# Two blocks of a language model on one core: another opening, index scores and gate panel moved, and marks that hold GpSimd

## The chip, the cores and the metric

The kernel runs on one core of a Trainium2 chip. The metric is the device time of one execution in microseconds (us), the median of the runs shown. All arithmetic is fp32; the large products are made of rounded halves, as told below.

## The reference

Input x has 512 tokens of 1024 features. Block 1 normalises x, projects it with w_in, and merges three branches: gated linear attention in chunks of 64, a causal convolution, and windowed attention. Block 2, run twice with weights of its own, has two branches: a gated recurrence (HGRN) and an attention over keys that a small indexer selects. Every block ends in a feed-forward part.

```
u = rmsnorm(x, g_mix);  z = u @ w_in                                  # block 1
y = sigmoid(gates) * (branches @ their own output weights);  h = x + merged @ w_o
# block 2, for each of two layers: z = rmsnorm(h) @ w_in_2
rel   = relu(einsum('bqhd,bsd->bqhs', rope(iq), rope(ik)))            # 4 index heads of 64
score = einsum('bqh,bqhs->bqs', iw, rel), causal
idx   = top_k(score, 128)                                             # per query
attn  = softmax(q k over idx) v,  q and k normed per head and roped
hgrn  = gated recurrence per head; rms over the head's 128 values, times silu(gate)
h    += (sigmoid(g1) * (attn @ w1) + sigmoid(g2) * (hgrn @ w2)) @ w_out
h    += (silu(h' @ w_a) * (h' @ w_b)) @ w_down,  h' = rmsnorm(h)
```

## The kernel before, in words

**Data.** Activations lie transposed, features on partitions (xT, 8 chunks of 128 x 512 tokens). Every operand of a large product is split in a high half (rounded to the format fp32r) and a low half (the rest), and a product is three matmuls: high x high, low x high, high x low. A weight panel is up to 2048 columns per partition (1 MB). The list of panels is written out by hand in weight_panels (line 190). SyncE loads a panel into one of three buffers raw when the panel that had the buffer has been used (line 917). ScalarE casts it to its high half wh (line 956) wherever its program calls ahead() (line 950); ahead() casts every further panel whose buffer's last user is an earlier pair than the one ScalarE has come to. GpSimd subtracts to get the low half wl, in four pieces of 512 columns, panel after panel in order (line 940). project (line 470) makes 48 matmuls of 128x512, 24 for each of two output chunks, into one of two PSUM pairs; a pair is free again when ScalarE or VectorE has read it. Each project can be cut in 4 steps of 12 matmuls.

**Opening.** x arrives as tokens, TensorE turns its 8 chunks (line 853), VectorE copies them to xT. ScalarE scales each chunk to the high half vh and squares it (squares, line 996), VectorE makes the low half vl_first (line 1500) and adds up squares (gather, line 1483 on). TensorE waits until all chunks are copied (line 858), then projects two panels from x scaled by the gains but not yet normalised (opening, line 535), and makes the column sums of the squares (sum_squares, line 518) behind the last chunk of the first panel. ScalarE's root and VectorE's reciprocal (line 1520) give scale. shadow (lines 1048 and 1535) then makes the normalised x chunk by chunk: VectorE scales a chunk (line 1538), ScalarE copies it to uh (line 1054), VectorE subtracts to get ul (line 1477). The first two panels' results are multiplied by scale as they are read (line 2075). The third panel (gla rank, gaT) and all others use uh and ul.

**Cores.** core (line 543) and core_chunked (line 620) run 8 units, each of 128 tokens and two heads. In a unit TensorE makes sums of log decays, ScalarE exponentiates them to dec (line 1082), VectorE multiplies dec with queries and keys for 7 levels (lines 1573 to 1581), TensorE multiplies levels (line 595), VectorE copies masked results to attT, and outputs and state follow. Between these, at five fixed slots of each unit, every engine takes steps of a side program (side_core_2 for block 2, 40 steps, 5 in a unit: slot 0 ahead of the second sums, slot 1 two steps ahead of the levels' matmuls, then slots 3 and 4). All engines have the same steps, so panels, pairs and reads line up. The side of block 2 projects the index key (IK), query and key panels with their norms and rotations, the index queries (IQ), values, and the first gate panel (HG).

**From core to attention in block 2.** TensorE makes index scores for the second and third query block (index, line 751) from PSUM pairs; ScalarE rectifies them into the one tile tmp[3] (indexed, line 1146), each time waiting until VectorE has used the last (score_keys, line 1878). core_post (lines 680, 1128, 1678) norms and gates the recurrence's heads in two halves, with steps of the merge (sigmoid gates and branch weights) between; the second gate panel is projected there, inside the merge's order. selection on VectorE is 16 rounds of max8 and match_replace for each of three query blocks (select, line 1897), 15 rounds ahead of the first gate, 10 ahead of the second, 23 spread over the attention, of which the last block's scores are made at its start.

## Time and profile before

| | us |
|---|---|
| median of 3 runs | 2701.91 (2696.97 to 2702.64) |
| profiled execution | 2704.65 |
| its span, first to last instruction | 2702.8 |
| TensorE busy | 2600.1 (96%) |
| VectorE, ScalarE, GpSimd busy | 1141.3, 992.8, 1076.9 |
| mean granted TensorE clock | 0.98 |

The stages of the execution begin at: first projection 26, first core 118, its attention 315, feed-forward 565, second block 933, its core 1004, attention 1242, feed-forward 1454, third block 1816, its core 1884, attention 2123, feed-forward 2335. In a row of the trace PE is TensorE, DVE VectorE, ACT ScalarE, POOL GpSimd; "L467" is the line; the time in brackets is how long the engine sat idle before it, and the arrow names what ended that.

### The profile page before, as it was taken

The page shows a single profiled execution, that of the slowest core. Times are in us where ns is not written, and L with a number is a line of the kernel's source. Part 1 is how long each engine was busy: PE and PEld are TensorE (multiplying, and loading weights), DVE is VectorE, ACT ScalarE, POOL GpSimd, SP SyncE. Part 2 cuts the span into 40 slices and gives each one's busy share as a digit, 9 for nine tenths or more (in the row PEclk, how much of TensorE's full clock was granted, in tenths as well). Part 3 has the DMA queues.
Part 4 walks back from the last instruction along what each step waited for, and adds up shares of the span by engine and source line. Part 5 has one row for each costly group of instructions (what it writes and reads, how often), then busy time and mean ns, then how long its engine had stood idle before and what let it go on. Part 6 is the DMA issues. An engine that isn't in the chain of part 4 may idle for free.

```text
span 2702.8 us, 30143 instructions
## 1 busy us (share of the span) xinstructions
PE 2600.1 (96%) x12482; PEld 2112.8 (78%) x12482; DVE 1141.3 (42%) x1977; ACT 992.8 (37%) x1126; POOL 1076.9 (40%) x816
## 2 busy tenths in 40 slices
PE   6998999999999999998999999999999899999998
PEld 4887777888888787876688888888787568888887
DVE  5343353355424466668634111133665863511112
ACT  3422542343323454434424222235443443422220
POOL 3333333645445443213253444443321325444442
PEclk9999999999999999988999999999998999999999
DMA  4222222222232221111132322233111112223222
GB/s 144 75 77 63 94 63 79 94 94 94 94 104 95 86 90 47 50 60 47 48 95 93 106 97 94 94 94 94 48 47 53 57 48 94 94 95 106 95 94 78
DMA packets 206708, 221.05 MB, mean 82 GB/s; under 512 B 3714, under 2 KB 197468, under 8 KB 206444
## 3 DMA queue, kind: packets, MB, share of 16 engines
q1 hardware_dynamic: 206064, 218.97, 25.4%
q8 instruction: 99, 1.62, 0.2%
q14 instruction: 38, 0.30, 0.0%
q10 hardware_dynamic: 507, 0.15, 0.0%
HBM read 217.01 MB, written 2.10 MB: 81 GB/s over the span
## 4 chain that ended last, share of the span: by engine, by line
PE 78%; DVE 14%; ACT 6%; issue 1%; DMA 0%; DVEq 0%; SPq 0%; ACTq 0%
PE psum L467 70%; PE psum L595 2%; DVE score L1902 2%; ACT wh L956 2%; DVE top L1900 2%; DVE ul L1775 1%; DVE tmp L1717 1%; DVE score L1890 1%; DVE dec L1581 1%; PE psum L713 1%; DVE ul L1477 1%; PE psum L574 1%; DVE merged L1798 1%; PE psum L575 1%; PE psum L725 1%
## 5 line engine op out<-in xcount | busy, mean ns | idle before, releaser
L940 POOL TENSOR_TENSOR wl<-raw,wh 128x512 fp32r<-128x512 f32 x812 | 1076.7, 1359 | 1600.0 <-ACT wh L956 1599.6
L467 PE MATMUL psum<-uh,wh 128*128 128x512 f32 x2024 | 811.0, 401 | 25.3 <-DVE ul L1775 4.3
L467 PE MATMUL psum<-ul,wh 128*128 128x512 f32 x2024 | 796.5, 394 | 0.0
L467 PE MATMUL psum<-uh,wl 128*128 128x512 f32 x2024 | 796.5, 394 | 0.0
L956 ACT CAST wh<-raw 128x2048 fp32r<-128x2048 f32 (+1 forms) x206 | 386.9, 1879 | 308.7 <-DMA raw<-in_w_ffn_out 118.1
L467 PEld LDWEIGHTS psum<-uh,wh 128*128 128x128 f32 x2024 | 385.7, 191 | 121.4 <-issue 19.3
L467 PEld LDWEIGHTS psum<-uh,wl 128*128 128x128 f32 x2024 | 385.1, 190 | 82.6
L467 PEld LDWEIGHTS psum<-ul,wh 128*128 128x128 f32 x2024 | 386.1, 191 | 78.5 <-issue 1.0
L467 PE MATMUL psum<-fh,wh 128*128 128x512 f32 x528 | 205.4, 389 | 0.0
L467 PE MATMUL psum<-fh,wl 128*128 128x512 f32 x528 | 205.4, 389 | 0.0
L467 PE MATMUL psum<-fl,wh 128*128 128x512 f32 x528 | 205.4, 389 | 0.0
L1817 DVE TENSOR_TENSOR xT<-xT,psum 128x1024 f32<-128x1024 f32 (+1 forms) x48 | 55.9, 1166 | 293.0 <-PE psum L467 292.8
L1863 DVE TENSOR_TENSOR tmp<-tmp,psum 128x1024 f32<-128x1024 f32 x22 | 26.9, 1221 | 358.6 <-PE psum L467 358.6
L467 PE MATMUL psum<-vh,wh 128*128 128x512 f32 x288 | 115.7, 402 | 9.6 <-DVE xT L2044 7.6
L467 PEld LDWEIGHTS psum<-fh,wl 128*128 128x128 f32 x528 | 99.1, 188 | 20.6
L467 PEld LDWEIGHTS psum<-fl,wh 128*128 128x128 f32 x528 | 99.1, 188 | 20.6
L467 PEld LDWEIGHTS psum<-fh,wh 128*128 128x128 f32 x528 | 99.1, 188 | 20.4
L467 PE MATMUL psum<-vh,wl 128*128 128x512 f32 x288 | 112.9, 392 | 0.0
L467 PE MATMUL psum<-vl,wh 128*128 128x512 f32 x256 | 99.7, 389 | 0.0
L467 PE MATMUL psum<-brh,wh 128*128 128x512 f32 x224 | 91.8, 410 | 1.7 <-ACT tmp L1154 1.7
L467 PE MATMUL psum<-brh,wl 128*128 128x512 f32 x224 | 89.1, 398 | 0.0
L467 PE MATMUL psum<-brl,wh 128*128 128x512 f32 x224 | 89.0, 397 | 0.0
(334 smaller groups left out, 3240.7 us busy)
## 6 DMA issues: line engine op xcount, KB each, us to landing
raw<-in_w_in SPq DMA_DIRECT2D x78, 1024.0 KB, 5.2
raw<-in_w_ffn_in SPq DMA_DIRECT2D x44, 1024.0 KB, 5.1
raw<-in_w_up SPq DMA_DIRECT2D x22, 1024.0 KB, 5.1
raw<-in_w_ffn_out SPq DMA_DIRECT2D x16, 1024.0 KB, 5.1
raw<-in_w_down SPq DMA_DIRECT2D x8, 1024.0 KB, 5.0
raw<-in_w_out SPq DMA_DIRECT2D x8, 1024.0 KB, 5.1
raw<-in_w_ffn_out SPq DMA_DIRECT2D x8, 768.0 KB, 4.4
raw<-in_w_o SPq DMA_DIRECT2D x4, 1024.0 KB, 5.0
```

The source lines that it names most:

```text
L467: ins = mm(dst, x, y, start=first and i == 0, stop=last and i == len(todo) - 1)
L574: mm(X[1 + b][:, 0:3 * P], lth[:, u % 2, i, :], summask[:, cols], start=True, stop=False)
L575: ins = mm(X[1 + b][:, 0:3 * P], ltl[:, u % 2, i, :], summask[:, cols], start=False, stop=True)
L595: ins = mm(level_scores(l)[:, i, :, :], dec[:, i, l, :], odd_blocks(dec[:, i, l, :], l), start=True, stop=True)
L713: ins = nc.tensor.transpose(X[2][:, c * P:(c + 1) * P], prob[i % 2][:, e, b * P:(b + 1) * P], ident)
L725: ins = mm(X[3][HD * e:HD * (e + 1), 0:P], vof(2 * p + e, b), probT[i % 2][:, e, (b - b0) * P:(b - b0 + 1) * P], start=(b == b0), stop=(b ...
L940: ins = nc.gpsimd.tensor_tensor(wl[p % 3][:, w], raw[p % 3][:, w], wh[p % 3][:, w].bitcast(F32), ALU.subtract)
L956: nc.scalar.copy(wh[p % 3][:, 0:nk * width], raw[p % 3][:, 0:nk * width]).then_inc(S.hi_done, 1)
L1477: v.tensor_tensor(dst, src, high.bitcast(F32), ALU.subtract).then_inc(sem, 1)
L1817: v.tensor_tensor(x, x, src, ALU.add).then_inc(pair_free[(n.q - 1) % 2], 1)
L1900: v.max(top8[:], sc).then_inc(S.dve_chain, 1)
L1902: v.match_replace(sc, top8[:], sc, TAKEN).then_inc(S.dve_chain, 1)
```

## The change

1. Opening: TensorE no longer waits for all copies; it follows the low halves chunk by chunk. ScalarE makes all high halves first, and squares behind them into four tiles; VectorE sums behind all low halves. The second panel is projected by project_high_first: its high matmuls (32), with the column sums between the two halves, then the 16 that need its low part, which GpSimd makes only behind the sums' additions. The third panel is unnormalised too.
2. Block 2: IQ comes right behind IK, the second gate panel right behind the first, out of the merge. Index scores of the second query block, their scoring and its 16 rounds move into the core's side; the third block's scores stay behind the core, in indexed_post, with 9 rounds. Rectified scores get more tiles, and every rectification is followed by ahead(). The first heads are squared and the first gate's SiLU made in the side's last step; the second gate's SiLU gets a tile of its own. Index weights are read by ScalarE in place of VectorE.
3. GpSimd: before the low part of some panels it waits for a mark (low_after): in the cores until VectorE has made its levels of the unit, in the output stage until the merged low halves are made.

```diff
-        for c in (C_HF, C_HQ, C_HF + 256, C_HQ + 256, C_HI, C_HI + 256,
-                  C_IK, C_AQ, C_AQ + 256, C_AK, C_AK + 256, C_IQ, C_AV, C_AV + 256, C_HG):
+                  C_IK, C_IQ, C_AQ, C_AQ + 256, C_AK, C_AK + 256, C_AV, C_AV + 256, C_HG, C_HG + 256):
-        merge(w, C_G2 + D, a["w_proj_hgrn_2"][l], C_HG + 256)
+        merge(w, C_G2 + D, a["w_proj_hgrn_2"][l])
...
-SIDE_CORE_2 = 2 + 4 * 5 + 4 + 5 + 5 + 4
+SIDE_CORE_2 = 2 + 5 + 4 * 5 + 5 + 4 + 4
-SIDE_POST_2 = (4, 2)
+SIDE_POST_2 = (2, 4)
-SELECT_EARLY = (15, 10)
+SELECT_CORE, SELECT_POST = (8, 8), 9
...
+            def hold_lows(first, sem):
+                for p in range(first, ended()):
+                    if p + 3 < n_panels:
+                        low_after[p + 3] = (sem, t.at[sem.name])
...
+            def project_high_first(xh, xl):
+                pe.wait_ge(S.hi_done, n.p + 1)
+                h, l = wview(wh, n.p), wview(wl, n.p)
+                n.p += 1
+                low_after[n.p - 1] = (S.n_part, DC // 2 - 1)
+                dst = new_pair()
+                for i, off in enumerate((0, P)):
+                    for k in range(DC):
+                        mm(dst[:, i, :], h[:, k, off:off + P], xh[:, k, :], start=(k == 0), stop=False)
+                        mm(dst[:, i, :], h[:, k, off:off + P], xl[:, k, :], start=False, stop=False)
+                    yield
+                pe.wait_ge(S.lo_done, n.p)
+                for i, off in enumerate((0, P)):
+                    for k in range(DC):
+                        ins = mm(dst[:, i, :], l[:, k, off:off + P], xh[:, k, :], start=False, stop=(k == DC - 1))
...
+                    hold_lows(free, S.lev_ready)
                     take_on(side, core_steps(total, u, 2))
                     take_on(side, core_steps(total, u, 3))
+                    free = ended()
...
+            def indexed_post(side, side_steps):
+                sum_heads()
+                finish(project(uh, ul))
+                index(2)
+                take_on(side, side_steps[0])
+                sum_heads()
+                take_on(side, side_steps[1])
+                pe.wait_ge(S.g_mean, t.up(S.g_mean, 2))
...
                 yield from project(uh, ul, (0,))
+                yield from project(uh, ul)
+                queries = n.q - 1
...
-            pe.wait_ge(S.x_copied, t.up(S.x_copied, 4))
-            opening(BARE_MIX_1, vl_first, DC - 1)
-            finish(project(uh, ul, (0,)))
+            n.fresh, n.sum_at, n.final = S.v_lo, None, False
+            finish(project(vh, vl_first))
+            second = project_high_first(vh, vl_first)
+            next(second)
+            sum_squares()
+            finish(second)
+            finish(project(vh, vl_first, (0,)))
+            n.fresh = S.n_lo
...
                 pool.wait_ge(S.hi_done, p + 1)
+                if p in low_after:
+                    pool.wait_ge(*low_after[p])
...
+            def rectify(m, j):
+                src = next_pair()
+                act.wait_ge(S.pair_full, n.q)
+                fn(index_tiles(m)[j], src[:, :, 0:(m + 1) * P], ACT.Relu).then_inc(pair_free[(n.q - 1) % 2], 1)
+                ahead()
+            def indexed_post(side, side_steps):
...
+                root_heads()
                 act.wait_ge(S.i_scored, t.up(S.i_scored))
+                inverse_root(tmp[2][:]).then_inc(S.g_root, 1)
+                silu_gate(silu1[:])
+                rectify(2, 0)
+                high_branch(0)
+                rectify(2, 1)
+                act.wait_ge(S.out_read, t.up(S.out_read))
+                square_heads(1)
+                take_on(side, side_steps[0])
+                root_heads()
...
+            def indexed_post(g, side, side_steps, selection):
+                gate_heads(0, g, True, tmp[0][:])
+                next_pair()
+                score_keys(2)
+                take_on(selection, SELECT_POST)
+                take_on(side, side_steps[0])
+                gate_heads(1, g, True, silu1[:])
+                take_on(side, side_steps[1])
...
+                score_keys(1)
                 yield
                 yield from wait_steps(2)
-                cosine(iq[:])
+                take_on(selection, SELECT_CORE[0])
                 yield
                 yield from passed(1)
...
+                yield from wait_steps(3)
+                next_pair()
+                take_on(selection, SELECT_CORE[1])
                 yield
...
             bare_low(DC // 2 - 1, gains(V_GMIX), vl_first)
-            opened = roots(gains(V_GMIX), BARE_MIX_1)
+            for s in range(DC // 2 - 1):
+                gather(s, first=True)
+            opened = roots(gains(V_GMIX), BARE_MIX_1, turns=(2, 3, 3))
             for j in range(2):
-                next(opened)
                 src = next_pair()
...
+                next(opened)
```

## Rows read from the trace of the kernel before

**Rows 1.** The page: the chain that ended last, by engine; one DMA issue's row.
```profile
PE 78%; DVE 14%; ACT 6%; issue 1%; DMA 0%; DVEq 0%; SPq 0%; ACTq 0%
...
raw<-in_w_in SPq DMA_DIRECT2D x78, 1024.0 KB, 5.2
```

**Rows 2.** Busy time by stretch: us, engines' busy, granted clock, DMA share, GB/s.
```profile
1004.00:1183.00 179.00, 170.75 (x998) 146.60 (x997) 110.57 (x268) 76.03 (x76) 48.96 (x36) 0.98 0.17 52
1183.00:1204.00 21.00, 15.12 (x50) 9.47 (x49) 11.41 (x24) 7.87 (x8) 5.34 (x4) 0.67 0.17 50
...
1454.00:1816.00 362.00, 362.00 (x1592) 298.72 (x1591) 70.17 (x68) 102.48 (x83) 167.07 (x132) 1.00 0.30 96
```

**Rows 3.** The chain of waits from 0 to 130: start, us, what.
```profile
17.41 1.33 ACT vh L1008 x2
...
20.54 0.70 DVE xT L2044
...
21.99 1.42 DVE vl_first L1500 x2
...
26.28 13.18 PE psum L467 x48
...
42.80 3.37 DVE scale L1520
...
50.00 1.24 DVE gk L2075
...
63.34 14.16 PE psum L467 x51
```

**Rows 4.** Timeline of ScalarE and GpSimd behind the reciprocal.
```profile
54.09 1.91 ACT L956 CAST wh<-raw 128x2048 fp32r<-128x2048 f32 x1
...
56.07 13.03 POOL L940 TENSOR_TENSOR wl<-raw,wh 128x512 fp32r<-128x512 f32 x8 [15.60 <-ACT wh L956]
```

**Rows 5.** Two cores: chain of waits, GpSimd's and VectorE's timeline; a TensorE wait.
```profile
1016.21 3.07 PE psum L595 x28
...
1026.78 2.75 PE psum L467 x12
...
1044.23 4.43 PE psum L595 x20
...
1033.35 10.48 POOL L940 TENSOR_TENSOR wl<-raw,wh 128x512 fp32r<-128x512 f32 x8 [13.23 <-ACT wh L956]
...
1042.62 1.35 DVE L1581 TENSOR_TENSOR dec<-dec,gq 128x128 f32<-128x128 f32 x1
...
1045.51 0.28 DVE L1581 TENSOR_TENSOR dec<-dec,gk 128x128 f32<-128x128 f32 x1
...
209.04 0.58 PE L657 MATMUL psum<-cdec 128*128 128x128 f32 x1 [2.10 <-DVE cdec L1643]
```

**Rows 6.** From the core to the attention: timelines, two selection stretches of VectorE, chain.
```profile
1184.99 0.70 PE L757 MATMUL psum<-ik,iq 64*128 64x256 f32 x4
...
1243.59 0.38 PE L702 MATMUL psum<-ak,aq 64*128 64x128 f32 x2 [1.63 <-DVE stat L1717]
...
1170.21 0.17 DVE L1569 COPY small<-dec 128x2 f32<-128x2 f32 x1 [8.14 <-ACT dec L1082]
...
1207.11 1.28 ACT L1119 ACT_TABLE_LOAD   x1
1208.40 1.06 ACT L1119 ACTIVATE tmp<-tmp 128x1024 f32<-128x1024 f32 x1
...
1199.50:1214.30 14.80, 13.77 (x46) 0.94 0.12 30
1223.30:1234.60 11.30, 10.64 (x27) 0.70 0.31 94
...
1228.43 1.01 ACT tmp L1116
...
1235.38 1.23 DVE tmp L1673
```

More of the change, by code:

```diff
@@ L461, in new_pair, with ended @@
                 return pair[(n.q - 1) % 2]
+            def ended():
+                return sum(1 for end in panel_end if end)
+            def hold_lows(first, sem):
+                for p in range(first, ended()):
+                    if p + 3 < n_panels:
+                        low_after[p + 3] = (sem, t.at[sem.name])
             def products(dst, terms, first, last):
@@ L558, in core @@
                     n.fresh = 0
+                free = ended() - 1
                 for u in range(CORE_UNITS):
@@ L630, in core_chunked @@
                 values = n.q - 1
+                free = ended() - 1
                 for u in range(CORE_UNITS):
@@ L777, in output @@
                 n.fresh = S.m_lo
-                residual(uh, ul)
+                last = ended() - 1
+                finish(project(uh, ul))
+                low_after[last + 3] = (S.m_lo, t.at["m_lo"])
+                for s in range(1, DC // 2):
+                    finish(project(uh, ul))
             def ffn(bare):
@@ L810, in side_core_2 @@
                 yield from project(uh, ul, (0,))
-                keys = n.q - 1
+                yield from project(uh, ul)
+                queries = n.q - 1
+                dst = new_pair()
+                mm(dst[:, 0, :], rot, ik[:], start=True, stop=True)
+                for m in range(NT):
+                    ins = nc.tensor.transpose(dst[:, 1, 4 * m:4 * m + 4], iwT[:, m * P:(m + 1) * P], ident[HD:HD + 4, HD:HD + 4])
+                ins.then_inc(S.pair_full, 1)
+                pe.wait_ge(pair_free[queries % 2], queries // 2 + 1)
+                turn(iq, rot)
+                yield
                 for j in range(4):
@@ L822, in side_core_2 @@
                     yield
-                yield from project(uh, ul)
-                queries = n.q - 1
-                dst = new_pair()
-                pe.wait_ge(pair_free[keys % 2], keys // 2 + 1)
-                for m in range(NT):
-                    nc.tensor.transpose(dst[:, 1, 4 * m:4 * m + 4], iwT[:, m * P:(m + 1) * P], ident[HD:HD + 4, HD:HD + 4])
-                mm(dst[:, 0, :], rot, ik[:], start=True, stop=True).then_inc(S.pair_full, 1)
-                yield
                 yield from project_tokens()
-                pe.wait_ge(pair_free[queries % 2], queries // 2 + 1)
-                turn(iq, rot)
+                index(1)
                 yield
@@ L994, in full, with squares @@
                 return 0
-            def squares(g, first=False, final=None):
+            def squares(g, final=None):
                 def square(s, i, inc):
@@ L1029, in squares, with first_squares @@
                     square(s, 0, last)
-                    if last and not first:
+                    if last:
                         act.wait_ge(pair_free[(n.q - 1) % 2], (n.q - 1) // 2 + 1)
                     square(s, 1, True)
-                    if not first:
-                        high(s)
+                    for c in (2 * s, 2 * s + 1):
+                        fn(vh[:, c, :], xT[:, c, :], ACT.Copy, scale=g(c)).then_inc(S.v_hi, 1)
                 t.up(S.n_part)
-                ahead(3 if first else n_panels, done=1)
+                ahead(done=1)
+            def first_squares(g):
+                ahead(1)
+                for s in range(DC // 2):
+                    act.wait_ge(S.x_copied, t.up(S.x_copied, 2))
+                    if s == 0:
+                        act.wait_ge(S.vec_ready, 1)
+                    for c in (2 * s, 2 * s + 1):
+                        fn(vh[:, c, :], xT[:, c, :], ACT.Copy, scale=vec[:, g + c:g + c + 1]).then_inc(S.v_hi, 1)
+                    if s == 1:
+                        ahead(2)
+                for s in range(DC // 2):
+                    last = s == DC // 2 - 1
+                    for i in range(2):
+                        ins = fn(tmp[(s + 2) % 4][:, i, :], xT[:, 2 * s + i, :], ACT.Square)
+                        if last or i == 1:
+                            ins.then_inc(S.n_square, 1)
+                t.up(S.n_part, DC // 2 - 1)
+                ahead(3, done=1)
             def roots(bare, final=False, turns=None):
@@ new lines, in gate_heads @@
+            def gate_heads(j, g, same, gate):
+                dve.wait_ge(S.g_root, t.up(S.g_root))
+                newton(tmp[1][:], tmp[2][:])
+                for i in range(2):
+                    col = g if same else g + 2 * j + i
+                    ins = v.scalar_tensor_tensor(tmp[3][:, i, :], gq[:, 2 * j + i, :], vech[:, col:col + 1],
+                                                 tmp[3][:, i, :], ALU.mult, ALU.mult)
+                ins.then_inc(S.dve_chain, 1)
+                dve.wait_ge(S.dve_chain, t.up(S.dve_chain))
+                v.tensor_tensor(tmp[3][:], tmp[3][:], gate, ALU.mult).then_inc(S.g_prod, 1)
+                dve.wait_ge(S.g_prod, t.up(S.g_prod))
+                dve.wait_ge(S.b_hi, t.up(S.b_hi))
+                low(brl[0][:, 2 * j:2 * j + 2, :], tmp[3][:], brh[0][:, 2 * j:2 * j + 2, :],
+                    S.branch_ready if j else S.g_split)
@@ L2191, in _ @@
                 dve.wait_ge(S.pair_full, n.q)
[L2192 removed]
+                selection = select_all()
+                core(1.0, side_core_2(l, selection), SIDE_CORE_2)
                 side = merge(early, first=True)
```

244 lines of the change are left out of this document (119 added, 125 removed).

## The prediction

> **What bounds the kernel now.** The chain of the whole span is read first: 78% of it is TensorE and 14% VectorE [rows 1]. Then the busy time by stage: in the second block's feed-forward TensorE works without a gap, 1592 matmuls in 362 us, 0.227 us each, at full clock; that is its floor. Neither the kernel's products nor their sizes are changed, so only gaps and slow-clock stretches can be won. The core of the second block has 8.3 us of gaps in 179, the 21 us behind it, in which the index scores are made, 5.9 of gaps and a granted clock of 0.67 [rows 2]. So three places are looked at: the opening, the recurrent core of the two indexed blocks (both behave alike, the first one's rows stand for both), and the stretch between that core and the attention. The profiled execution took 2704.65 us, 1.85 more than its span; the median of the three runs shown is 2701.91, 2.7 below it.
>
> **Opening, before.** The first 48 products start at 26.28, when all of x has been turned and copied, and take 13.18; sums and square root follow, and the reciprocal ends at 46.17 [rows 3]. Then VectorE and ScalarE make the normalised x chunk by chunk while GpSimd makes two panels' low parts, 13.03; the 51 matmuls from 63.34 on take 14.16, 2.6 more than at 0.227 [rows 3, 4].
>
> **Opening, after.** TensorE starts at the first low half. VectorE's order from 18.24 is low pair, copies, low pair, copies, low pair, low pair: 4 x 1.42 + 4 x 0.70 = 8.5, the last chunk at 26.8 [rows 3]. TensorE needs 48 x 0.227 = 10.9 from about 19.0 and ends near 30.2; if it restarts at the lower clock (13.18 instead of 10.9, [rows 3]), near 32.5. ScalarE makes four pairs of high halves (4 x 1.33) and one weight cast (1.91) from 17.41, so to 24.6, and then eight squares, at the price of a high half 5.3: 29.9. The last additions on VectorE follow within 1.5. Sixteen high products (3.6) bring TensorE to 33.8, so it waits for none of this. Column sums and root took 39.46 to 42.80, 3.3, and the reciprocal 3.37: 40.5, which is 5.6 earlier. The second and third panels (32 and 24 products, 7.3 and 5.4 us) end near 49. The cast of the fourth panel began 7.9 after the reciprocal (54.09 less 46.17, [rows 4]); now one more scaling of a PSUM pair (1.24, [rows 3]) is ahead of it: 49.7, cast to 51.6. Its low part is half of a burst that took 13.03 for two panels: 6.5, so 58.1 [rows 4]. **What is late next** is thus GpSimd's low part of the fourth panel; TensorE sits idle for 9 us ahead of it, as it now does in short pieces, and starts at 58.1 in place of 63.34, with the same slow start. Gain **5.1**, from 3 (slow restart at 19.0, 2.3 less) to 6.5 (less slow clock behind).
>
> **Core of an indexed block.** In its second unit GpSimd makes 8 pieces in 10.48 us. While it runs, each 128x128 multiplication of VectorE takes 1.35, whatever its size, one per GpSimd piece; the level matmuls, 3.07 in the first unit, last until 1048.66 here, 19.1 behind the projection's end at 1029.5 [rows 5]. The changed panel order puts the index queries here. ScalarE copies them and casts one panel before the second exponential, so GpSimd still has one burst here, 4 pieces, not held: its mark was set a unit earlier. It starts 3 us after the query panel and ends near 8.3. The second burst's panel is cast in this unit and waits for the levels. VectorE's first level operations lose three pieces, the others run free, and the levels end near 11 in place of 16.3 (1045.8 less 1029.5). TensorE leaves the level matmuls 7.2 earlier (11.9 instead of 19.1, by [rows 5] and 3.07 for the uncontended group), and I allow 1.3 for slow clock behind them (20 of the 28 matmuls took 4.43 there, twice their share of 3.07). That is 8.5. Against it: index scores of the second query block (two pairs, 0.70 each, [rows 6]) move into the core, 1.4; in unit 7 the rectification lets TensorE wait about 0.7; and I allow 0.5 for selection. Selection: 16 rounds move into two places on VectorE behind the state updates. A round on 256 keys costs 14.8 / 15 = 0.99 [rows 6], eight 7.9; VectorE sits idle 8.14 us before the last unit [rows 6], which is what hides the first eight, with nothing to spare. The last eight run 5.9 us into the next stage, where VectorE waits for a root anyway. Net **5.9** per block; 3 if the levels are still contended by both bursts half the time, 8 if nothing new is paid.
>
> The marks on the queue of GpSimd also stand in the first block's core. There a panel is cast at the pass two panels after its slot's last user, a unit later than the mark that holds it. By this count the stalls there (2.10 at 209.04, [rows 5]) stay: **0**. In the output stage only the third panel's low part is held, which is cast as the last low half is being made: 0.
>
> **Between core and attention.** From the core's last product (1184.99) to the second query-key product (1243.59) it is 58.6 us [rows 6]. ScalarE's chain of SiLU, cast, four rectifications that each wait for VectorE, and then 15 rounds of selection (14.8) stand ahead of the first head gate; TensorE's own work is 144 products (32.7) and some 7 of small ones, by the 0.70 of a pair. After, counted from the core's last product: TensorE sums heads (1.4, by the two pairs of index scores) and does the gate panel (10.9) to 12.3. ScalarE: SiLU with its table load 2.4, a cast 4.3, and from the mean to the gate's start 6.9 (1228.43 to 1235.38, [rows 6]): 11.2. VectorE then gates the first heads, done well before 19. ScalarE waits for the gate panel: SiLU to 14.7, cast 16.6, rectification 17.4. **Here a new wait arises**: the moved rectification also casts ahead, and that panel's load is issued only at 12.3 and lands 5.2 later [rows 1], so the cast ends at 19.5 and the copy that VectorE waits for at 20.6. Behind it on ScalarE are the second rectification and the squares. VectorE: low half, four scorings and the mask against GpSimd's bursts (a piece of about 1.3 each) to 27.6; nine rounds on 384 keys, 11.3 [rows 6], to 38.8; from the second gate's start to the second query-key product it is 8.2 (1235.38 to 1243.59, [rows 6]): 47.0. TensorE needs about 43 and waits, and the second query-key product stands at 47. So **11.6** are gained, VectorE and not TensorE still setting the end; 7 if the panels' bursts also hit the second gate, 14 if the cast is not late.
>
> ScalarE's table loads: the row shows 1.28, and the activation starts 0.01 behind it [rows 6]. One such load stands on this path behind the gate panel. The Trainium skill (ScalarE: Activation LUTs, What ACT_TABLE_LOAD costs) adds a drain of about 1.38 us to each switch; with that the sum would be 2 x 1.38 = 2.8 us later. The trace shows no such gap.
>
> **Start of the attention.** ScalarE's two rectifications no longer wait for VectorE, but now a cast stands between them, and two GpSimd bursts in place of one run beside VectorE's four scorings. By the same count VectorE is ready 1.3 later than now and TensorE 0.9: **0.9 lost** per block, between 3 lost and 1.5 gained. The rounds left for the attention are 48 - 16 - 9 = 23, as before (48 - 25).
>
> **Sum.** 5.1 + 2 x (5.9 + 11.6 - 0.9) = 38.3. The profiled execution would be 2666.4, the median **2663.6 us**. With all low ends (3 + 2 x 7) it is 2685, with all high ends (6.5 + 2 x 23.5, not all together) about 2648. A measurement of this kernel tells a change from none at about 0.2%, 5 us.
>
> **Rivals.** (a) The post stage stays as crowded as it is: bursts of GpSimd cover more of VectorE's two-tensor operations, and the second query-key product comes at 54, not 47. For it: four two-tensor operations there cost a piece each; against: selection, the largest part, took 11.3 with GpSimd busy beside it, so it isn't touched. 2 x 7 less gain: 2678. Chance 0.20. (b) The marks do work in the first block: the stall at 209.04 and its twin go, each 2.1 and as much again of slow clock and late start, an estimate of 7: 2657. Against: my count of units. 0.10. (c) The gain between core and attention is given back, because VectorE's chain through the attention is as long as before and TensorE only waits later: 2663.6 + 23 = 2687. Against: rounds in the attention are unchanged, and 16 of the others went where VectorE was idle. 0.07. (d) **Slower**: GpSimd's queue is in order, so a held low part holds all behind it. If in each of the 16 units of the two cores TensorE reached its next panel before the burst (10.48 / 2 = 5.2) was done, it would pay 16 x 5.2 = 83: about 2747. It decides only where a panel's low part is ready less than a hold ahead of its use. The burst of 1033 to 1044 serves panels whose products start 21 us later and more, and a hold ends with the levels of the same unit, at most about 10 us. 0.03. (e) The new opening does nothing because the second panel's data or the sums are late: 2668.7, within my own range; counted with the forecast. The forecast itself: 0.60.
>
> **Numbers.** From these: faster by over 0.2% 0.94 (forecast, a, b, most of c), within 0.2% 0.03 (the tail of c and of the forecast), slower 0.03 (d). Range 2643 to 2685: from 5 below the high ends, for (b) with good ends, to the low ends; it leaves out (c) and (d), 0.10, and tails of the rest.
>
> **What would show it.** Right: first projection product near 19, reciprocal's end near 40.5, fourth panel's products from 58; one 4-piece burst beside the levels of the second unit, then levels of 3 us; 8 rounds ending just at the last unit's copy of the decay; from the core's end to the second query-key product 47 us, ended by VectorE; ScalarE waiting for a load between two rectifications. Wrong: TensorE waiting for low parts inside the cores, the copy of the decay late by several us in the last unit, or an attention stage longer by more than 3 us.

## The result, and the profile after

The changed kernel takes 2669.76 us (median of 4 runs, 2666.36 to 2674.41), the kernel before 2701.0 in the same comparison (2696.97 to 2702.64): a ratio of 0.9882, 95% interval 0.9864 to 0.9899. The forecast was 2663.6, range 2643 to 2685, so the sign and the range held, and the gain was forecast 7.1 us, about a quarter, too large: 38.3 us against 31.2 between the medians. The profiled execution spans 2667.0 against 2702.8 before. The two traces side by side (all times in us from the span's start; the core's end is the first product behind the core's last unit):

```
place                                  before    after    moved   forecast
fourth panel's first product            63.34    58.20     -5.1     -5.1
first core's first sums                120.57   116.95     -3.6     -5.1
first attention's first product        315.82   308.16     -7.7     -5.1
second block's core, first sums       1006.00   995.37    -10.6     -5.1
that core's end                       1184.99  1171.88    -13.1    -11.0
its second query-key product          1243.59  1219.94    -23.7    -22.6
third block's core, first sums        1885.94  1863.45    -22.5    -21.7
its second query-key product          2124.04  2086.75    -37.3    -39.2
last transposes                       2693.24  2657.41    -35.8    -38.3
```

**Opening.** Timelines of the changed kernel (start, us, what, and in brackets the idle time ahead with the one that ended it), to be read beside [rows 3, 4]:

```profile
37.35 3.35 DVE L1629 RECIPROCAL scale<-root 128x512 f32<-128x512 f32 x1 [7.18 <-ACT root L1114]
...
49.90 1.89 ACT L1022 CAST wh<-raw 128x2048 fp32r<-128x2048 f32 x1
...
51.87 6.28 POOL L1006 TENSOR_TENSOR wl<-raw,wh 128x512 fp32r<-128x512 f32 x4 [11.56 <-ACT wh L1022]
...
58.20 0.80 PE L487 MATMUL psum<-uh,wh 128*128 128x512 f32 x1 [8.95 <-POOL wl L1006]
...
72.15 4.82 PE L930 MATMUL psum<-gaT,walpha 16*128 16x512 f32 x8
```

The reciprocal ends at 40.70, and TensorE stands for 8.95 us before a panel whose low half is not made yet. Behind it the 48 products and the eight small ones of alpha (the last row) run at a granted clock of 0.78 and 0.75.

**Second unit of the indexed core.** Timelines of GpSimd, VectorE and TensorE in the changed kernel, against [rows 5], where one burst of eight pieces lay over all the level factors:

```profile
1021.83 5.36 POOL L1006 TENSOR_TENSOR wl<-raw,wh 128x512 fp32r<-128x512 f32 x4 [11.57 <-ACT wh L1022]
1030.11 5.00 POOL L1006 TENSOR_TENSOR wl<-raw,wh 128x512 fp32r<-128x512 f32 x4 [2.92 <-DVE dec L1690]
...
1025.97 1.37 DVE L1690 TENSOR_TENSOR dec<-dec,gq 128x128 f32<-128x128 f32 x1
1027.26 0.28 DVE L1690 TENSOR_TENSOR dec<-dec,gk 128x128 f32<-128x128 f32 x1
...
1027.59 3.34 PE L636 MATMUL psum<-dec 128*128 128x64 f32 x28 [0.16 <-DVE dec L1690]
```

Four pieces, then the factors at 0.28 each, then, released by the last of them, four more pieces. From unit to unit it is 23.1 us in place of 30.6.

**Between core and attention, and the attention's start.** ScalarE, VectorE, GpSimd and TensorE in the changed kernel, against [rows 6]:

```profile
1187.43 0.81 ACT L1232 ACTIVATE rectified<-psum 128x768 f32<-128x768 f32 x1
1189.74 1.91 ACT L1022 CAST wh<-raw 128x2048 fp32r<-128x2048 f32 x1 [1.49 <-DMA raw<-in_w_proj_hgrn]
1191.56 1.05 ACT L1212 CAST brh<-tmp 128x1024 fp32r<-128x1024 f32 x1
...
1192.71 2.28 DVE L1586 TENSOR_TENSOR brl<-tmp,brh 128x1024 fp32r<-128x1024 f32 x1 [5.65 <-ACT brh L1212]
...
1187.61 11.44 POOL L1006 TENSOR_TENSOR wl<-raw,wh 128x512 fp32r<-128x512 f32 x8 [7.51 <-ACT wh L1022]
...
1219.94 0.80 PE L759 MATMUL psum<-ak,aq 64*128 64x128 f32 x4 [6.63 <-DVE stat L1835]
...
1232.71 0.48 PE L779 MATMUL psum<-const,inverse 128*128 128x128 f32 x1 [4.06 <-DVE inverse L1856]
```

From the core's end to the second query-key product it is 48.1 us in either block. ScalarE waits for a load between two rectifications, VectorE 5.65 us for the copy behind it, and TensorE at the end 6.63 us for VectorE.

### The profile page after: what moved, and what is told of

Same layout as the page of the kernel before. It is cut to its first block, busy times and chain, and to the rows that moved or that the text cites. A ratio compares the mean times of both kernels' runs of the same rounds, so it can differ in the third digit from the quotient of the medians.

```text
span 2667.0 us, 30163 instructions
## 1 busy us (share of the span) xinstructions
PE 2573.2 (96%) x12482; PEld 2093.8 (79%) x12482; DVE 1143.3 (43%) x1973; ACT 995.8 (37%) x1132; POOL 1074.3 (40%) x816
## 4 chain that ended last, share of the span: by engine, by line
PE 83%; DVE 9%; ACT 5%; DMA 1%; issue 1%; POOL 0%; DVEq 0%; SPq 0%; ACTq 0%
PE psum L487 73%; ACT wh L1022 2%; PE psum L636 1%; PE psum L770 1%; PE psum L782 1%; PE psum L759 1%; DVE ul L1893 1%; DVE score L2002 1%; DMA raw<-in_w_in 1%; DVE merged L1916 1%; PE psum L615 1%; PE psum L616 1%; PE psum L888 0%; DVE ul L1586 0%; PE psum L866 0%
## 5 line engine op out<-in xcount | busy, mean ns | idle before, releaser
L487 PE MATMUL psum<-uh,wh 128*128 128x512 f32 x2016 | 800.5, 397 | 26.6 <-POOL wl L1006 8.9
L487 PE MATMUL psum<-uh,wl 128*128 128x512 f32 x2016 | 787.3, 391 | 0.0
L487 PE MATMUL psum<-ul,wh 128*128 128x512 f32 x2016 | 786.9, 390 | 0.0
L487 PEld LDWEIGHTS psum<-uh,wh 128*128 128x128 f32 x2016 | 379.8, 188 | 116.8 <-issue 18.2
L487 PEld LDWEIGHTS psum<-uh,wl 128*128 128x128 f32 x2016 | 379.6, 188 | 80.6
L487 PEld LDWEIGHTS psum<-ul,wh 128*128 128x128 f32 x2016 | 380.1, 189 | 77.4 <-issue 1.4
L487 PE MATMUL psum<-brh,wh 128*128 128x512 f32 x224 | 91.9, 410 | 0.0
```

What stands on the lines that cost most here:

```text
L487: ins = mm(dst, x, y, start=first and i == 0, stop=last and i == len(todo) - 1)
```

## The experiments

Each ratio is to the kernel before, run in the same comparison; medians are set against the 2669.76 of the changed kernel. "Unit" is the distance from one unit's first sums to the next's. The median of the kernel before lies between 2701.0 and 2704.3 from comparison to comparison; by the ratios the distances from the changed kernel are, from E1 to E10, +3.5, +16.2, -17.6, -8.1, +31.3, +5.4, -5.9, -23.0, -9.2 and -35.1 us. The intervals of E1, E4, E6, E7 and E9 overlap with the changed kernel's own, so what these five show rests on their traces.

**E1, the old opening put back.** VectorE's and ScalarE's parts of it, left out here, go back with it.

```diff
-            finish(project(vh, vl_first))
-            second = project_high_first(vh, vl_first)
...
-            finish(project(vh, vl_first, (0,)))
+            opening(BARE_MIX_1, vl_first, DC - 1)
+            finish(project(uh, ul, (0,)))
...
-            first_squares(V_GMIX)
+            old_squares(lambda c: vec[:, V_GMIX + c:V_GMIX + c + 1], first=True)
```

> The changed kernel with the opening of before put back; all else stays changed. The alpha products began 5.3 us earlier after the change, but took 4.8 us in place of 3.7, and the first core began 3.6 us earlier. Theory A (the opening's gain is kept to the end): 3.6 to 5.3 us over the changed kernel, some 2674.5. Theory B (the granted clock or a later wait gives it back before the first core ends): within 1 us of it, 2670. Theory C (the shift also moves the phase of later bursts and so bought the further 4 us that the first core gained): some 8 us over, 2678, and then the first attention's first query-key product is at its old place, 315.8, and no longer at 308.2.

Measured: 2675.65, ratio 0.9895 (0.9875 to 0.9915), 5.9 us over the changed kernel by the medians and 3.5 by the ratios (0.13%), with intervals that overlap. The first core begins at 121.39, 4.4 later. That is theory A, within what can be measured. The first query-key product stands at 316.85, as C said; but C's reason, bursts in another phase, is not what the traces show. Here is the stretch from the first core's first sums to that product, before the change and after it (length, TensorE's busy time first; the granted clock is the number behind the five engines):

```profile
120.57:315.82 195.25, 188.06 (x886) 155.02 (x887) 76.07 (x138) 70.55 (x74) 69.72 (x56) 0.97 0.23 72
116.95:308.16 191.21, 184.03 (x886) 151.54 (x886) 76.36 (x138) 70.59 (x74) 69.46 (x56) 1.00 0.24 73
```

TensorE has the same 886 products and idles for 7.2 us in both; the 4.0 us lie in its busy time alone, at a granted clock of 0.97 and 1.00. E1 has 195.5 at 0.97. The runs that share the new opening and the same products there have 191.2 at 1.00 (changed kernel, E2, E5), 192.6 and 192.9 at 0.99 (E4, E9), 194.1 and 194.3 at 0.98 (E6, E3). Some 3 of the 4 us are thus no more than one execution differs from another. Whether the old opening, whose two profiles are the longest, makes the low clock likelier is not shown.

**E2, no marks in the cores.**

```diff
                     if p + 3 < n_panels:
-                        low_after[p + 3] = (sem, t.at[sem.name])
+                        pass
```

> The changed kernel without the marks that hold GpSimd's low halves behind the levels in either core (the marks of the opening and of the output projection stay). Theory A (the marks are what shortened the second unit of each indexed core from 30.6 to 23.1 us: the second burst of low halves waited for the levels): that unit grows back by 3.5 to 7.5 us, the kernel by 7 to 15, some 2681. Theory B (the shorter unit comes from the index panel's new place, which moved the casts and so the bursts, and the marks do nothing): within 1 us of 2670. In the first core both theories expect no change, since the stalls there stood with the marks too.

Measured: 2688.66, ratio 0.9942 (0.9922 to 0.9961), 19 over (16 by the ratios). Theory A; more than it allowed. GpSimd's and VectorE's timelines of this run, second unit, and TensorE's chain of waits there:

```profile
1025.17 10.45 POOL L1005 TENSOR_TENSOR wl<-raw,wh 128x512 fp32r<-128x512 f32 x8 [19.44 <-ACT wh L1021]
...
1034.42 1.35 DVE L1689 TENSOR_TENSOR dec<-dec,gq 128x128 f32<-128x128 f32 x1
1035.69 0.28 DVE L1689 TENSOR_TENSOR dec<-dec,gk 128x128 f32<-128x128 f32 x1
...
1036.02 4.53 PE psum L635 x20
1040.55 4.49 PE psum L486 x12
```

The two bursts are one again, the factors take 1.35 until it ends, and the unit takes 30.2 and 30.4 us in the two blocks against 23.1: nearly all of before's 30.6. So all of the change but the marks gives some 0.5 there, the marks 7.2. In the rows above slow clock follows, 0.55 granted from 1036 to 1045: 12 projections take 4.49 where [rows 5] have 2.75. First and seventh units are longer too (26.2 and 21.2 for 19.6, 24.6 for 23.1). Of these only the 26.2 can be put down in part to the marks: four factors of that unit take 1.35 to 1.38 beside a burst that is held in the changed kernel, TensorE waits 2.22 for a masked copy, and its granted clock is 0.80. The 21.2 is at 0.92 and the 24.6 at 0.93 without any further wait, and runs that have the marks show the same (21.0 at 0.92 in E7, 24.7 at 0.93 in E5). In the first core nothing changed, as both theories had it.

**E3, no cast ahead of the first gate's high half.**

```diff
-                silu_gate(silu1[:])
-                rectify(2, 0)
+                silu_gate(silu1[:], cast=False)
+                rectify(2, 0, cast=False)
                 high_branch(0)
                 rectify(2, 1)
```

> The changed kernel, but behind each indexed core ScalarE casts no panel between the second gate's silu and the high half of the first gate's product (two casts go behind it). DVE waited 5.65 us there for that high half, 2.65 of them behind a cast of 1.9 and a DMA wait of 1.5. Theory A (DVE's chain sets the second query-key product, PE had 6.6 us of slack): the high half comes some 4.6 us earlier, the product some 4 us earlier in each of two blocks, so 2662. Theory B (the panels cast later reach PE later, and PE takes over the bound): 0 to 2 us per block, 2667 to 2670. Theory C (the low halves on GpSimd, now later, run beside the scoring and slow it, and then the attention's start): no gain, 2670 or slightly over.

Measured: 2654.92, ratio 0.9817 (0.9795 to 0.9839), 14.8 under. ScalarE, GpSimd, VectorE, TensorE:

```profile
1190.14 1.05 ACT L1213 CAST brh<-tmp 128x1024 fp32r<-128x1024 f32 x1 [0.63 <-DVE tmp L1798]
1191.10 0.81 ACT L1233 ACTIVATE rectified<-psum 128x768 f32<-128x768 f32 x1
1191.80 3.71 ACT L1022 CAST wh<-raw 128x2048 fp32r<-128x2048 f32 x2
...
1193.78 10.76 POOL L1006 TENSOR_TENSOR wl<-raw,wh 128x512 fp32r<-128x512 f32 x8 [10.65 <-ACT wh L1022]
...
1191.29 1.23 DVE L1588 TENSOR_TENSOR brl<-tmp,brh 128x1024 fp32r<-128x1024 f32 x1 [1.19 <-ACT brh L1213]
1197.17 0.56 DVE L2014 MAX8 top<-score 128x8 f32<-128x384 f32 x1
...
1216.64 0.49 PE L759 MATMUL psum<-ak,aq 64*128 64x128 f32 x4 [1.12 <-DVE stat L1837]
```

From core's end to this product it is 41.7 in both blocks, 6.4 less, and the attention keeps it: from there to its last value product it is 93.9, against 94.3. Theory A, and more than its 4, because the burst that began at 1187.61 now begins at 1193.78 and leaves the low half (1.23 in place of 2.28) and part of the scoring alone. TensorE's slack is down to 1.1: it nearly takes over the bound, as B feared.

**E4, the fourth panel cast at once behind the root.**

```diff
             opened = roots(BARE_MIX_1, turns=(2, 3, 3))
+            ahead(4, done=2)
             next(opened)
             finish(passed(1))
             next(opened)
-            ahead(4, done=1)
```

> The changed kernel with the fourth panel's cast moved from behind the fifth chunk of the normed x to right behind the root, where ScalarE has nothing to do. PE waited 8.95 us for this panel's low halves (until 58.20). Theory A (the cast's place alone made the wait): the low halves are there by 47 to 50, the fourth panel is bound by the last chunks of the normed x, begins near 50 and ends near 65 in place of 72.2; the first core begins 5 to 8 us earlier, 2662 to 2665. Theory B (the burst now runs beside DVE's chunks of the normed x and slows them, at 0.75 to 1.6 us for each product): the last chunk moves from 58 to 60 or later, and the gain is 1 to 3 us. Theory C (given back at the alpha products, whose inputs or whose sigmoid and setup chain on DVE come no earlier): within 1 us of 2670.

Measured: 2665.28, ratio 0.9852 (0.9831 to 0.9874), 4.5 under. GpSimd, TensorE (alpha, then a later panel), ScalarE:

```profile
35.29 10.95 POOL L1006 TENSOR_TENSOR wl<-raw,wh 128x512 fp32r<-128x512 f32 x8
...
60.85 0.69 PE L930 MATMUL psum<-gaT,walpha 16*128 16x512 f32 x1
...
92.41 0.58 PE L487 MATMUL psum<-wh,uh 128*128 128x256 f32 x1 [3.34 <-POOL wl L1006]
...
75.94 0.63 ACT L1484 ACTIVATE sinT<-tmp 128x512 f32<-128x512 f32 x1 [10.87 <-DVE tmp L2242]
```

The alpha products come 11.3 earlier, so A is right about the wait. But the first core begins at 109.17, 7.8 earlier than in the changed kernel's profile and 3.7 to 5.1 earlier than in those of E2, E3, E6, E7 and E9 (112.9 to 114.3). So less than the 11.3 arrives. What gives the rest back is part of C: ScalarE cannot pass the sines, for which VectorE's setup ends at 75.9, so its later casts are late, and TensorE waits 3.34 for a low half at 92.4.

**E5 and E6, selection moved.**

```diff
-SELECT_CORE, SELECT_POST = (8, 8), 9
+SELECT_CORE, SELECT_POST = (0, 0), 25      (E5)
+SELECT_CORE, SELECT_POST = (8, 8), 4       (E6)
```

> The changed kernel with the 16 selection rounds of the core put back behind it (none within the last two units, 25 between the two gates, the late ones unchanged). Theory A (DVE's chain from the core's end to the second query-key product sets that product, and the rounds in the core are nearly free): the stretch grows from 48.0 by 16 rounds of 0.98 and one bias of 1.1, so 16.8 us, to some 64.8 in each block; the core gives back 1 to 2 us per block; together 2669.8 + 2 x 15.3 = 2700. Theory B (the rounds cost as much within the core, since PE waits for DVE there too): the kernel is longer by 5 us or less.

> The changed kernel with 4 selection rounds between the gates in place of 9; the other 5 go to the late ones, 28 in place of 23 over eleven head pairs of the attention. Theory A (the stretch to the second query-key product loses the 5 rounds of 1.25 us, as PE waited 6.6 us there, and the attention takes them into DVE's gaps): 2 x 6.2 us less, 2657. Theory B (DVE is 95% busy in the attention's first third and 92% in the second, beside a PE as busy, so the rounds are given back there): the second query-key product comes 6.2 us earlier in each block, the last value product at most 2 us; 2666 to 2670.

E5: 2704.04, ratio 0.9998 (0.9986 to 1.0009). The stretch takes 64.1 in both blocks, 16.1 more, and TensorE waits at its end:

```profile
1237.42 0.80 PE L759 MATMUL psum<-ak,aq 64*128 64x128 f32 x4 [22.76 <-DVE stat L1835]
```

Theory A, and the core gives nothing back: its seventh unit takes 24.7 here at a granted clock of 0.93; with the rounds it is 23.1 at 1.00 in the changed kernel's profile and again 24.7 at 0.93 in E3's. The 16 rounds in the core are free, and having them there is worth as much as the whole change brings.

E6: 2675.11, ratio 0.9902 (0.9887 to 0.9917); not below the changed kernel, and above the 2666 to 2670 that theory B allowed. The trace is theory B's: the second query-key product comes 41.8 behind the core's end, 6.3 less, with 0.22 of waiting left, and from there to the last value product it is 101.1 in place of 94.3, 6.8 more (5.5 more in the third block). VectorE's busy time (third of the engines) in one stretch of that attention, first E6, then the changed kernel:

```profile
1260.00:1290.00 30.00, 27.45 (x161) 18.51 (x160) 28.58 (x80) 13.22 (x31) 5.00 (x4) 0.94 0.12 37
1260.00:1290.00 30.00, 28.74 (x174) 19.79 (x173) 27.42 (x82) 14.30 (x34) 5.01 (x4) 1.00 0.12 37
```

VectorE is busy for 28.6 of 30 us where it was 27.4, and TensorE does 161 products where it did 174, a part of it by a granted clock of 0.94 in place of 1.00.

**E7, two marks of the first core a unit later.**

```diff
                     hold_lows(free, S.lev_ready)
                     free = ended()
+                    if u in (4, 6):
+                        low_after[free + 2] = (S.lev_ready, t.at["lev_ready"] + 2)
```

> The changed kernel with the marks of two panels of the first core set to the levels of the unit in which they are cast (the sixth and the eighth), not of the unit in which their buffer came free. PE waited 0.68 and 2.10 us there, and 1.79, for level factors that DVE made at 1.1 to 1.35 us each beside GpSimd's four pieces, in place of 0.28 to 0.42. Theory A (the marks did nothing in the first core because they were released one unit early): the three waits go, 4.6 us, and up to 3 of slow clock behind them; 2662 to 2665. Theory B (the burst only moves on, and slows the gate and convolution work behind it, so that a later wait takes their place): within 1.5 us of 2670.

The rows of the changed kernel that it speaks of (GpSimd, VectorE, TensorE):

```profile
199.93 5.21 POOL L1006 TENSOR_TENSOR wl<-raw,wh 128x512 fp32r<-128x512 f32 x4 [11.69 <-ACT wh L1022]
...
202.68 1.35 DVE L1751 TENSOR_TENSOR cdec<-cdec,gq 128x128 f32<-128x128 f32 x1
203.95 1.34 DVE L1752 TENSOR_TENSOR cdec<-cdec,gk 128x128 f32<-128x128 f32 x1
...
205.35 0.49 PE L701 MATMUL psum<-cdec 128*128 128x128 f32 x2 [2.10 <-DVE cdec L1752]
```

and of E7:

```profile
199.00 0.29 DVE L1753 TENSOR_TENSOR cdec<-cdec,gq 128x128 f32<-128x128 f32 x1
199.20 0.29 DVE L1754 TENSOR_TENSOR cdec<-cdec,gk 128x128 f32<-128x128 f32 x1
...
200.31 6.19 POOL L1008 TENSOR_TENSOR wl<-raw,wh 128x512 fp32r<-128x512 f32 x4 [14.71 <-DVE cdec L1748]
```

Measured: 2663.53, ratio 0.9860 (0.9846 to 0.9875), 6.2 under. TensorE has no wait at all between 195 and 240; the one of 2.20 at the core's end, for the last state, stays as in every kernel here. The sixth unit takes 14.9 in place of 18.0, and from the first sums to the first attention it is 187.4, 3.8 less than the shortest of the runs with the marks a unit earlier or without them. Theory A.

**E8, five edits at once.** E3, E4 and E7 together, and `cast=False` in two more places:

```diff
-                rectify(1, 0)
+                rectify(1, 0, cast=False)
...
-                    rectify(NT - 1, 0)
+                    rectify(NT - 1, 0, cast=False)
```

> The changed kernel with five edits at once: the casts behind the indexed cores moved behind the first gate's high half, the fourth panel's cast right behind the root, the two marks of the first core a unit later, and, new here, both rectifications of the first scoring in the core, and of the last one at the attention's start, ahead of the casts between them. If the parts add up: 14.8 for the first, 4.5 for the second by their runs, some 5 for the third, and for the last 1.85 (the wait at 1146.49) and up to 1.9 (the cast ahead of the second rectification, before the wait of 4.06 at 1232.71) in each of two blocks, 3 to 7: 2669.8 - 14.8 - 4.5 - 5 - 5 = some 2640. Rival (casts later than before leave PE waiting for panels in the core's last unit or in the attention, or the granted clock falls): 2650 or over.

Measured: 2645.71, ratio 0.9797 (0.9783 to 0.9812), 24.1 under: what E3, E4 and E7 give added up (14.8 + 4.5 + 6.2 = 25.5), and nothing for the two new places, where I had expected 3 to 7. By the ratios the parts would be 31.6 and the whole is 23.0, so the sum alone decides little; the trace does. The seventh unit still takes 23.0, and from the second query-key product to the first inverse it is 12.8, as in the changed kernel. TensorE's waits and VectorE's steps there in E8:

```profile
1136.80 0.49 PE L650 MATMUL psum<-attT,gv 128*128 128x128 f32 x2 [1.71 <-DVE attT L1708]
1216.65 0.38 PE L781 MATMUL psum<-const,inverse 128*128 128x128 f32 x1 [4.05 <-DVE inverse L1860]
...
1129.02 3.32 DVE L2006 SCALAR_TENSOR_TENSOR score<-tmp,iw,score 128x256 f32<-128x256 f32 x3
...
1210.81 3.33 DVE L2006 SCALAR_TENSOR_TENSOR score<-rectified,iw,score 128x512 f32<-128x512 f32 x2
1214.17 1.23 DVE L2009 TENSOR_TENSOR score<-score,const 128x128 f32<-128x128 f32 x1
1215.63 0.97 DVE L1860 COPY inverse<-stat 128x128 f32<-128x128 f32 x1
```

My theory that the casts made these waits fell. The bursts lay beside the scoring all the same.

**E9 and E10, the bursts held behind the scoring.** E9 is the changed kernel with this alone, E10 is E8 with it:

```diff
+                    if u == 6:
+                        low_after[ended() + 2] = (S.pairs_done, t.at["pairs_done"] + 1)
...
                     index(NT - 1)
+                    for p in (ended() + 1, ended() + 2):
+                        low_after[p] = (S.inverted, t.at["inverted"] + 1)
```

> The changed kernel with two more marks and nothing else. GpSimd's burst in the unit of the first scoring waits for that unit's mask copies, and the two bursts at the attention's start wait for the first inverse. Both times ScalarE's cast was blamed for PE's waits (1.85 at 1146.49, 4.06 at 1232.71), but the kernel with all casts moved kept them (1.71 and 4.05): there the burst began earlier and DVE's scoring steps of 128x256 took 1.1 in place of 0.48, those of 128x512 took 1.67 in place of 0.67. Theory A (the burst beside the scoring makes these waits): the wait in the core falls to 0.5 or less and that at the attention's start to 1 or less, up to 5 us per block, 2660 to 2663. Theory B (the chain of ScalarE's rectifications and casts makes them, the slower scoring is hidden): within 1.5 us of 2670.

> The kernel with the five edits (2645.7 measured) and the two marks of the run before in addition. Here the rectifications come ahead of the casts, so only the bursts are left to make the two waits of 1.71 and 4.05 us. Theory A: both go, 4.5 to 5.5 us per block, 2635 to 2637. Theory B (the burst held is late for PE, which then waits for the panel in the attention): within 2 us of 2646 or over it.

E9: 2661.84, ratio 0.9848 (0.9831 to 0.9866), 7.9 under. The seventh unit takes 21.0 in both blocks (2.0 to 2.1 less), the whole core 173.4 and 173.3, and from the second query-key product to the last value product it is 91.9, 2.3 less. The wait at the inverse falls from 4.06 to 0.96. Theory A. E10: 2635.73, ratio 0.9752 (0.9738 to 0.9765), 10.0 under E8. The same steps in E10, and GpSimd's burst behind them:

```profile
1130.49 1.53 DVE L2010 SCALAR_TENSOR_TENSOR score<-tmp,iw,score 128x256 f32<-128x256 f32 x3
...
1209.21 1.54 DVE L2010 SCALAR_TENSOR_TENSOR score<-rectified,iw,score 128x512 f32<-128x512 f32 x2
1210.79 0.29 DVE L2013 TENSOR_TENSOR score<-score,const 128x128 f32<-128x128 f32 x1
1211.31 0.23 DVE L1864 COPY inverse<-stat 128x128 f32<-128x128 f32 x1
...
1211.68 9.99 POOL L1012 TENSOR_TENSOR wl<-raw,wh 128x512 fp32r<-128x512 f32 x8 [20.38 <-DVE inverse L1864]
```

Both waits are gone, and no panel held by these marks is late; the 3.12 us that TensorE waits for a low half at 92.5 belong to E4's edit. E10 is the fastest kernel here: 67 us below the one before, 34 below the changed one.

## Why the prediction was right, and where its sizes were off

**Opening.** Right step by step as far as the fourth panel's start: start at 19.11 (about 19.0), reciprocal's end 40.70 (40.5), GpSimd's low part late next, start of the fourth panel 58.20 (58.1). What failed is the clause that the fourth panel and all behind it run as before: the alpha products took 4.82 in place of 3.7, at a granted clock of 0.75, and 3.6 of the 5.1 reached the first core in this execution. E1 puts the opening's worth at 3.5 to 6, E4 shows what it left undone.

**First core.** The count of units was right: the marks there are released a unit early, the stall of 2.10 stood in the changed kernel, E2 changed nothing in it, and E7 moved two marks and took the stalls away. Rival (b) fell for the reason given, and its price, 7, was near what the repair brought (6.2). That the stretch lost 4.1 us all the same was not forecast, and it is the granted clock (0.97 before, 1.00 after), as the rows beside E1 show. Another 3.0 were gained between the first attention and the second core. They are the clock as well. Two places behind pauses of TensorE that are the same in both kernels (2.74 and 2.75, 2.11 and 2.24 us) have a low clock before and a full one after; the first of them, before and after:

```profile
450.00:454.00 4.00, 4.00 (x12) 3.15 (x11) 2.45 (x2) 0.93 (x1) 0.00 (x0) 0.57 0.00 1
442.35:446.35 4.00, 4.00 (x19) 3.32 (x18) 2.45 (x2) 0.95 (x1) 0.00 (x0) 1.00 0.00 1
```

The second has 0.62 at 610 to 614.5 before, and 1.00 after. The profiles of E3, E7 and E9, whose code is the changed kernel's in this stretch, have one or two such places again and need 690.5, 689.7 and 692.6 us for this stretch, where before took 690.2 and the changed kernel 687.2. From the first core's first sums to the second core's it is 884.8 and 885.5 us in E3 and E9, 885.4 before and 878.4 in the changed kernel: the whole 7.0 is within what executions of the same code differ by, and no run shows that the change made any of it.

**Indexed core.** Forecast 5.9 less per block, measured 2.5 in the second block (179.0 to 176.5) and 4.2 in the third (179.5 to 175.3). The second unit was right: 8.5 forecast, 7.5 measured, and E2 showed the mechanism, two bursts kept apart by a mark. The step that was mis-sized is the one on index scores that move into the core: 1.4 + 0.7 + 0.5 = 2.6 forecast, against 3.9 by the last three units (66.6 in place of 62.7). Two things are in it. The sixth unit takes 22.4 in place of 20.2, and TensorE has no gap in either: the new order puts the column sums of a norm there (3.3 us of products where 0.9 were), which the forecast did not count. In the seventh (1.8 more) I had priced the moved work on TensorE and a wait for the rectification, but not VectorE's scoring beside a burst: the masked copies came late, and TensorE waited 1.85. E8 showed that it isn't the cast, E9 that it is the burst: with it held, the core is 5.6 and 6.2 shorter than before, about the 5.9 of the forecast. The remaining 1.1 in this block is one unit that took 23.1 and not 22.1; in the third block it took 22.1. Selection in the core cost nothing measurable (E5), against 0.5 forecast.

**Between core and attention.** Forecast 47.0, measured 48.1, ended by VectorE, with the late load between two rectifications in its place (19.5 for the cast's end, measured 19.8). The gain per block is 10.5 for 11.6. E5 and E3 confirm the chain: 16 rounds more lengthen it by 16.1, a cast and its wait less shorten it by 6.4. Rival (a) fell; the second gate's steps took 1.22 each, free of bursts. The rule of the Trainium skill weighed there (ScalarE: Activation LUTs, What ACT_TABLE_LOAD costs), a drain of about 1.38 us at each switch of tables, would have put the product an estimated 2.8 later; the loads still show none (load at 1178.32 for 1.28, activation at 1179.61).

**Attention.** Its start lost 1.2 to 1.3 per block (0.9 forecast), by VectorE's scoring beside two bursts. Rival (c), that the gain is given back in VectorE's chain, fell for this change: from the second query-key product to the last value product it is 94.3, and was 93.1. But E6 showed its mechanism in the neighbouring case: rounds that enter the attention are paid there in full. Its counter-argument, that the rounds in the attention are unchanged, was the one that decides.

**Slower.** Rival (d), TensorE waiting for held low parts, appears nowhere in the cores, not even in E10, which holds the most.

The sum came out near because misses cancel, and in part by luck. In the profiled pair the opening kept 1.5 less than forecast, the two indexed cores gave 3.4 and 1.7 less, the stretches behind them 1.1 less each, and the attentions took 0.3 and 0.6 more: together some 9.5. Against this stand 7.0 that came unforecast between the first core's sums and the second core's, by a granted clock that E3's and E9's executions of the same code did not have. The median moved less than the profiled pair (31.2 against 35.8), since the profiled execution of before was slower than its median and that of the changed kernel was not.

## What to carry to other kernels

When GpSimd works beside VectorE, look at when its burst starts, not at how long it takes: put it behind the steps that another engine waits for. Marks in its queue did this for 7 us per block with nothing else changed, and each such mark has to name the stage in which its input is made, not the one in which its buffer came free. A step moved to hide it is free only where its engine has true idle time at that spot: 16 rounds in the core cost nothing, 5 rounds in the attention cost about all they saved. And a wait that names one engine may be made by another's contention; an edit that takes the suspect away, as E8 did, tells them apart.

## What the runs showed of the hardware

A VectorE operation with two inputs from SBUF takes 0.6 to 1.1 us more while a burst runs, nearly whatever its size: 128x128 takes 1.35 (0.28 alone), 128x256 1.1 (0.48 to 0.51 alone), 128x512 1.67 (0.75 alone), 128x1024 2.28 (1.23 alone). For the small ones that comes to about one GpSimd piece of 1.25 to 1.35 each, as the forecast counted; for the large ones it is more than a piece. Small operations lose most. This is what the Trainium skill states (SBUF — State Buffer, section SBUF: two separate sides): the port pair that the two engines share is locked for a whole instruction, and the loser waits in full. The trace agrees, since what is added stays below the length of one piece. What I had not expected is that some operations with one input pay as well: the copy of the inverse took 0.97 beside a burst and 0.23 without, and the first scoring step of 128x512 0.67 against 0.49; the same page names operations in a two-port mode, which no run here tests by itself. The search for the eight largest isn't touched: 0.56 for 384 keys beside the burst of E3 and without one.

The granted clock of TensorE after a stretch of idling varies between executions of the same code. Behind the same wait of 8.9 us and the same 48 products, the alpha products took 4.82 in the changed kernel's profile at a granted clock of 0.75, so at 1.2 GHz for half of the time, 4.85 in E5's, and 3.7 in those of E2, E3, E6, E7 and E9, all of it at the full 2.4 GHz in E7's. Over the whole first core and its way to the attention this is worth 191.2 to 194.3 us, with the same waits. Three microseconds of difference in one stretch of two single profiles are therefore not evidence, unless the waits or the order of the rows differ too.
